# Two trunk layers with a mixture of experts on one core: gate and up by column tile, the gated rows transposed by VectorE

## What is computed

```python
def moe_ffn(h, router_w, router_bias, w_gate, w_up, w_down):
    ...
    hg = jnp.einsum('td,edf->tef', t, w_gate)
    hu = jnp.einsum('td,edf->tef', t, w_up)
    act = jax.nn.silu(hg) * hu * comb[:, :, None].astype(t.dtype)
    return jnp.einsum('tef,efd->td', act, w_down).reshape(B, L, D)
```

## Time and profile before

| | us |
|---|---|
| median of 3 runs | 1427.08 (1424.84 to 1427.25) |
| the profiled execution | 1437.77 |
| its span, first to last instruction | 1436.1 |
| TensorE busy in the span | 1110.4 (77%) |
| VectorE busy | 438.6 (31%) |
| ScalarE busy | 248.4 (17%) |
| GpSimd busy | 109.1 (8%) |
| HBM traffic over the span | 343.57 MB, mean 239 GB/s |

### The profile page before, as it was taken

One profiled execution on the slowest core, in us unless ns is written; L12 is line 12 of the kernel. 1 busy time (PEld: TensorE's weight loads), 2 busy tenths in 40 slices (PEclk: granted clock), 3 DMA queues, 4 the chain that ended last, 5 costly groups with the idle time before them and its releaser, 6 DMA issues.

```text
span 1436.1 us, 24771 instructions
## 1 busy us (share of the span) xinstructions
PE 1110.4 (77%) x9756; PEld 627.9 (44%) x9757; DVE 438.6 (31%) x1120; ACT 248.4 (17%) x456; POOL 109.1 (8%) x168
## 2 busy tenths in 40 slices
PE   1899996885579686889479998989739789877650
PEld 0444455535335343445245554444525455444320
DVE  0310137645112111222354233641522122222116
ACT  0301023303012111112221111110212121211101
POOL 1100000100100000001120000000010000000002
PEclk9999998995789888999889997989759999999975
DMA  9965233592575999781994015337322727599973
GB/s 325 366 226 201 99 125 133 222 381 113 225 306 223 419 422 422 323 322 41 387 375 160 35 59 202 121 118 292 118 95 83 327 95 301 217 408 415 421 315 132
DMA packets 96965, 343.57 MB, mean 239 GB/s; under 512 B 9926, under 2 KB 19081, under 8 KB 88732
## 3 DMA queue, kind: packets, MB, share of 16 engines
q1 hardware_dynamic: 69396, 289.19, 51.3%
q0 software_dynamic: 13152, 42.92, 8.4%
q10 hardware_dynamic: 14376, 10.89, 2.5%
HBM read 319.73 MB, written 23.23 MB: 239 GB/s over the span
## 4 chain that ended last, share of the span: by engine, by line
PE 47%; DMA 22%; DVE 11%; issue 10%; ACTq 5%; ACT 2%; SPq 2%; POOL 1%; DVEq 0%; POOLq 0%
PE bank L573 10%; DMA slot_rows<-arena 10%; PE bank L825 9%; PE bank L754 6%; PE bank L696 6%; ACTq L1068 5%; DMA arena<-in_moe_w_up_dram 4%; DMA ring<-in_ada_w_dram 4%; PE bank L739 4%; DMA ring<-in_moe_w_down_dram 3%; PE bank L748 2%; PE bank L526 2%; DVE arena L1160 1%; DVE arena L1141 1%; SPq L1176 1%
## 5 line engine op out<-in xcount | busy, mean ns | idle before, releaser
L739 PE MATMUL bank<-ring,arena 128*32 128x256 f32 x3008 | 198.2, 408 | 36.2 <-issue 24.2
L1063 ACT ACT_TABLE_LOAD x67 | 86.0, 1283 | 385.7 <-issue 370.8
L573 PE MATMUL bank<-ring,hT 128*128 128x512 f32 x336 | 144.9, 593 | 1.0 <-ACT hT L958 1.0
L739 PEld LDWEIGHTS bank<-ring,arena 128*32 128x32 f32 x3008 | 97.5, 116 | 110.0 <-issue 58.7
L748 PE MATMUL bank<-keep,arena 128*128 128x64 f32 x536 | 91.0, 294 | 64.1 <-DVE arena L1141 64.0
L825 PE MATMUL bank<-hT,ring 128*128 128x384 f32 x384 | 124.6, 487 | 1.0 <-ACT hT L958 1.0
L748 PEld LDWEIGHTS bank<-keep,arena 128*128 128x128 f32 x536 | 72.7, 197 | 110.3 <-DVE arena L1141 105.7
L739 PE MATMUL bank<-arena 128*32 128x256 f32 x1280 | 86.5, 416 | 17.7 <-DMA arena<-in_moe_w_up_dram 17.7
L573 PEld LDWEIGHTS bank<-ring,hT 128*128 128x128 f32 x336 | 63.6, 190 | 80.5 <-issue 79.3
L526 PE MATMUL bank<-ring,small 128*32 128x256 f32 x768 | 56.5, 459 | 53.4 <-DMA ring<-in_ada_w_dram 52.7
L754 PE MATMUL bank<-ring,arena 128*32 128x256 f32 x1504 | 95.0, 395 | 2.5 <-DMA ring<-in_moe_w_down_dram 2.5
(11 more groups left out here) (287 smaller groups left out, 1083.4 us busy)
## 6 DMA issues: line engine op xcount, KB each, us to landing
ring<-in_ada_w_dram SPq DMA_DIRECT2D x24, 2048.0 KB, 13.9
ring<-in_moe_w_gate_dram SPq DMA_DIRECT2D x22, 2048.0 KB, 17.2
ring<-in_moe_w_up_dram SPq DMA_DIRECT2D x22, 2048.0 KB, 16.7
ring<-in_moe_w_down_dram SPq DMA_DIRECT2D x22, 2048.0 KB, 20.4
arena<-in_moe_w_gate_dram SPq DMA_DIRECT2D x10, 2048.0 KB, 20.0
arena<-in_moe_w_up_dram SPq DMA_DIRECT2D x10, 2048.0 KB, 24.9
arena<-in_moe_w_down_dram SPq DMA_DIRECT2D x10, 2048.0 KB, 26.1
ring<-in_ev_w_in_dram SPq DMA_DIRECT2D x7, 2048.0 KB, 15.9
```

Of the source, the lines that this page charges most:

```text
L573: last = pe.matmul(bank[3 * (c % 2) + t], hT[:, k, t * P:(t + 1) * P], slot8(n)[:, k, :], start=k == 0, stop=k == KT - 1)
L739: last = pe.matmul(bank[1 + half][tile * BLK:(tile + 1) * BLK, 0:HALF], slot_inT[:, odd, pair, :], w[:, 2 * pair + odd, half * HALF:(half ...
L1063: act.activation(silu_g[:, 2 * half:2 * half + 2, :], bank[3 + half][:, 0:4 * BLK].rearrange("p (f s) -> p f s", f=2)[:, :, 0:BLK], ACT.Si ...
```

## The change

Each column tile of TensorE now takes 128 features of its own, both gate and up, over all eight groups of channels: a matmul's 256 columns are 128 of gate and 128 of up, from two places of the ring (`pair_of`). All of a block's gate and up is in bank 1, with nothing to add up afterwards: row 32 q + s has features 128 q to 128 q + 127 of slot s. ScalarE takes Silu of the whole 128 x 128 in one instruction, reading the features in the order (f, r) with feature = 128 q + 4 r + f. VectorE multiplies, and transposes the product in blocks of 32 x 32 (L1128 of the changed kernel), twice 128 x 64. Feature 128 q + 4 r + f then lies on partition 32 q + r, so w_down is now laid out `(p k) n` as well: partition p takes the 4 rows that lie next to each other. The copies of the 128 x 256 rows, the matmuls with `sides` and the constant itself are gone. `rows_in` now comes behind both halves of `gated`.

```diff
             src = a[("moe_w_gate", "moe_w_up", "moe_w_down")[j]][layer].rearrange("e d f -> (e d) f")
             rows = D if j < 2 else 512
-            src = src[bass.ds(e * rows, rows), :].rearrange("(p k) n -> p k n" if j < 2 else "(k p) n -> p k n", p=P)
+            src = src[bass.ds(e * rows, rows), :].rearrange("(p k) n -> p k n", p=P)
...
-            def gate_and_up(s, half, pair):
-
-                for side, w in enumerate((slot8(s), slot8(s + 1))):
-                    for odd in range(2):
-                        tile = 2 * side + odd
-                        last = pe.matmul(bank[1 + half][tile * BLK:(tile + 1) * BLK, 0:HALF], slot_inT[:, odd, pair, :],
-                                         w[:, 2 * pair + odd, half * HALF:(half + 1) * HALF], start=pair == 0, stop=pair == 3)
+            def gate_and_up(s, k):
+
+                both = pair_of(s)
+                for q in range(4):
+                    last = pe.matmul(bank[1][q * BLK:(q + 1) * BLK, 0:HALF], slot_inT[:, k % 2, k // 2, :],
+                                     both[:, :, k, q * P:(q + 1) * P], start=k == 0, stop=k == KT - 1)
                 return last
-
-            def features(b, half):
-
-                pe.wait_ge(S["gu_out"], b * 2 + (half + 1))
-                for f in range(2):
-                    at_f = half * HALF + f * P
-                    last = pe.matmul(bank[3 + half][:, f * 2 * BLK:(f + 1) * 2 * BLK], gu_rows[:, at_f:at_f + P], sides, start=True, stop=True)
-                last.then_inc(S["guT_mm"], 1)
...
                 pe.wait_ge(S["rowT"], b + 1)
-                for pair in range(4):
-                    last = gate_and_up(s, 0, pair)
+                for k in range(KT):
+                    last = gate_and_up(s, k)
                 last.then_inc(S["gu_mm"], 1)
-                gate_and_up(s, 1, 0)
-                gate_and_up(s, 1, 1)
-                features(b, 0)
-                gate_and_up(s, 1, 2)
-                gate_and_up(s, 1, 3).then_inc(S["gu_mm"], 1)
                 rows_to_channels()
-                features(b, 1)
...
-                for half in range(2):
-                    act.wait_ge(S["guT_mm"], b * 2 + (half + 1))
-                    act.activation(silu_g[:, 2 * half:2 * half + 2, :],
-                                   bank[3 + half][:, 0:4 * BLK].rearrange("p (f s) -> p f s", f=2)[:, :, 0:BLK],
-                                   ACT.Silu).then_inc(S["silu"], 1)
+                act.wait_ge(S["gu_mm"], b + 1)
+                act.activation(silu_g, bank[1][:, 0:P].rearrange("p (r f) -> p f r", f=FT), ACT.Silu).then_inc(S["silu"], 1)
...
-            def rows_out(b, half):
-                dve.wait_ge(S["gu_mm"], b * 2 + (half + 1))
-                dve.tensor_copy(gu_rows[:, half * HALF:(half + 1) * HALF], bank[1 + half][:, 0:HALF]).then_inc(S["gu_out"], 1)
-
             def gated(b, half):
-                up = bank[3 + half][:, 0:4 * BLK].rearrange("p (f s) -> p f s", f=2)[:, :, BLK:2 * BLK]
-                dve.wait_ge(S["silu"], b * 2 + (half + 1))
-                dve.tensor_tensor(act_T[:, 2 * half:2 * half + 2, :], silu_g[:, 2 * half:2 * half + 2, :], up, ALU.mult).then_inc(S["act"], 1)
+                up = bank[1][:, P:2 * P].rearrange("p (r f) -> p f r", f=FT)[:, 2 * half:2 * half + 2, :]
+                two = slice(2 * half, 2 * half + 2)
+                dve.tensor_tensor(act_rows[:, two, :], silu_g[:, two, :], up, ALU.mult).then_inc(S["gated"], 1)
+                dve.wait_ge(S["gated"], b * 2 + (half + 1))
+                dve.transpose(act_T[:, two, :].rearrange("p f s -> p (f s)"),
+                              act_rows[:, two, :].rearrange("p f s -> p (f s)")).then_inc(S["act"], 1)
...
             with dve.Fori(0, blocks) as b:
-                rows_out(b, 0)
+                dve.wait_ge(S["silu"], b + 1)
                 gated(b, 0)
-                rows_out(b, 1)
+                gated(b, 1)
                 dve.wait_ge(S["rowT_mm"], b + 2)
                 rows_in()
-                gated(b, 1)
```

More of the change, by code:

```diff
@@ L91 @@
 SLOT, FULL, PREVIOUS = ring_slots()
-K_ID, K_TRI, K_ONE, K_KEYG, K_KEYE, K_WF, K_LEFT, K_J, K_SIDE = 0, 128, 256, 384, 388, 404, 407, 408, 409
-K_N = 473
+K_ID, K_TRI, K_ONE, K_KEYG, K_KEYE, K_WF, K_LEFT, K_J = 0, 128, 256, 384, 388, 404, 407, 408
+K_N = 409
 M_RELF, M_RELB, M_MF, M_MB, M_XI, M_XB, M_RC, M_RS, M_DC, M_DS = (
@@ L116, in constants @@
     keep[:, K_J] = i
-    for side in range(2):
-        for s in range(BLK):
-            keep[[2 * side * BLK + s, (2 * side + 1) * BLK + s], K_SIDE + side * BLK + s] = 1
     mix = np.zeros((P, M_N))
@@ L209, in trunk_program @@
         ones = keep[:, K_ONE:K_ONE + P]
-        sides = keep[:, K_SIDE:K_SIDE + 2 * BLK]
         xf = x[:, :, :].rearrange("p t d -> p (t d)")
@@ L267, in trunk_program @@
         slot_inT = at(3328, 2, 4, BLK)
-        gu_rows = at(3584, 512)
-        silu_g = at(4096, FT, BLK)
+        silu_g = at(3584, FT, BLK)
+        act_rows = at(3712, FT, BLK)
         act_T = at(4224, FT, BLK)
@@ L349, in trunk_program @@
         MS = [{n: sem(f"{n}_{layer}") for n in (
-            "row_in", "rowT_mm", "rowT", "gu_mm", "gu_out", "guT_mm", "silu", "act", "down_mm", "slot_evac",
+            "row_in", "rowT_mm", "rowT", "gu_mm", "silu", "gated", "act", "down_mm", "slot_evac",
             "slot_stored")} for layer in range(2)]
@@ L406, in slot4, with pair_of @@
             return slot_of(n).rearrange("p (k n) -> p k n", k=FT)
+        def pair_of(n):
+            s = SLOT[n]
+            two = ring[:, s:s + 2, :].rearrange("p w c -> p (w c)") if s < RING else at(SPARE + (s - RING) * CHUNK, 2 * CHUNK)
+            return two.rearrange("p (w k n) -> p w k n", w=2, k=KT)
         def expert_matrix(sp, layer, e, s, j):
@@ L1181, in expert_through @@
                 if j < 2:
-                    sp.wait_ge(MS[layer]["gu_mm"], ends * 2)
+                    sp.wait_ge(MS[layer]["gu_mm"], ends)
                 else:
```

## The result

The changed kernel takes 1435.40 us (median of 8 runs, 1431.68 to 1439.59), the kernel before 1427.16 (8 runs, 1424.84 to 1428.37): a ratio of 1.0061, 95% interval 1.0044 to 1.0078, so **slower by 0.6%**, 8 us. The forecast was 1422.5: inside the range, on the wrong side. The profiled execution took 1439.59 us, with a span of 1437.8, 4.2 above its median.

What follows compares the result with a forecast made beforehand. Taken as bound: in quiet blocks a closed loop through stores, table load and Silu, in loaded blocks slow stores. Terms -14.3, -3, +21.2 and -8.5 sum to -4.6 us, giving a median of 1422.5; range 1403 to 1437.

Steps and rivals of the forecast that it cites:

- The closed loop of the quiet block: Blocks with no weights loading: eviction, stores, table load, Silu, `down`, eviction; 0.62 us less each, -14.3 us over 23.
- the whole new block: New order inside the expert blocks: -14.3 us in quiet blocks, -3 us in blocks that TensorE paces.
- rival 1: Slow stores also hold up the ring's refills, stretching the loading, and the kernel gets slower: 1433.5 us; chance 0.22.
- The pace: Every expert block under a long stretch of weight loading takes 12.1 us, its stores being slow throughout.
- The last block: End of layer 1, waiting for its down matrix: 10.6 us instead of 19.1, -8.5 us.
- Rivals 2 and 3: Stores as fast as now, 1401 us, chance 0.14; or VectorE's transpose dear, 1436.8 us, chance 0.04.
- rival 3: VectorE's transpose costs 0.85 us with its wait, so quiet blocks gain nothing: 1436.8 us; chance 0.04.
- rival 4: The weights set the end anyway; quiet-block gains turn into waiting for the next matrix: 1427 us; chance 0.10.
- the term on down's packets: w_down in 16 KB pieces slows stores in four long stretches of loading: +21.2 us; its load itself costs nothing.
- Short bursts of three matrices: Blocks beside brief loads of three matrices keep their times, their one store being slow already: put at nothing.
- The long stretches: Four runs of blocks under loading, from 460, 1110, 1242 and 1310 us: +9.7, +1.2, +4.0, +6.3, together +21.2 us.
- the five blocks from 1242: A stretch of loading late in the kernel: 10.5 us, three blocks at 12.1, one at 6.9, so +4.0 us.

Runs made afterwards that it cites:

- the control: The kernel before, unchanged, run and profiled once more: 1426.30 us, ratio 0.9991.

## Why the prediction was wrong

**What held.** The closed loop of the quiet block: each of its steps came within 0.05 us, and with the 4 KB pieces back the quiet blocks gave -13.4 for a forecast -14.3, the whole new block 15.8 us in the total for a forecast 14.3 + 3. The packets: w_down in 16 KB is served like gate and up, and its load alone costs nothing (the loading from about 457 to 602 us ends at the same time, so rival 1's stretched refills didn't come, although its 1433.5 lies within 2 us of the result). The pace: eleven blocks from 461.96 to 594.76 take 12.07 us each, forecast 12.1. The last block took 8.4 us, forecast 10.6, and q1 had 1.51 MB beside 0.44 on q0 from 1384 to 1389 us, 77% for a forecast four fifths. That down landed at 1389.6, forecast 1385 to 1390, is partly luck: it was issued at 1358.8, 5 us later than before and not up to 4 earlier, and landed 30.8 us after that instead of 39.7. The last two row vectors on q0 were issued only at 1387.2 and 1387.8, before at 1379.0 and 1379.5, 14 us ahead of the landing. Rivals 2 and 3 fell by the slow stores and the 0.24 us transpose, although rival 3's 1436.8 lies nearest of all to the result; of rival 4 nothing showed, as what was won in quiet blocks stayed won.

**What failed** is one sentence of the term on down's packets: "Short bursts of three matrices keep their times, since their one slow store is slow already." A burst (gate, up and down of one expert; the one of 620.7 us has landed at 639.1) outlasts a loaded block of 12 us, and its down part is now 16 KB pieces too. The first block's stores in it landed in 7.8 us in the median and 8.8 at most in the kernel before (issued from 614 to 621 us), and in 8.5 and 10.6 now (from 624 us). The block that starts at 624.25 us went from 10.8 to 12.6, and the two from 1292 from 10.4 and 7.5 to 12.0 and 11.7 us.

Two blocks behind a burst, quiet before (7.6 each), took 9.2 and 9.5, and not by a store's landing. In the first of them:

```profile
438.86 0.42 DVE L1142 COPY arena<-bank 128x256 f32<-128x256 f32 x1 [2.13 <-DMA slot_rows<-arena]
439.46 2.72 ACTq L1052 DMA_DIRECT2D slot_rows<-arena  x4
...
444.67 3.25 PE L747 MATMUL bank<-ring,arena 128*32 128x256 f32 x32 [1.74 <-DVE arena L1128]
...
448.09 0.42 DVE L1142 COPY arena<-bank 128x256 f32<-128x256 f32 x1 [2.78 <-PE bank L747]
```

Issuing the four stores takes 2.72 us (2.94 in the other block) instead of 1.75, which moves Silu, and `down` takes 3.25 (3.31) instead of 1.93. TensorE's clock for this `down` and for that of the quiet block above (bounds, length, busy, clock, DMA share, GB/s):

```profile
444.67:447.92 3.25, 3.25 (x36) 0.58 0.11 40
664.52:666.45 1.93, 1.93 (x36) 1.00 0.22 68
```

The 0.58 is a mean between the clock's two levels, near the lower (1.2 of 2.4 GHz). The engine had stood idle for 1.04 us and for 1.74 us before this `down`. The first is a wait for rows fetched on q0, of which the prediction said that they are "wanted a block later". Together the two effects are the 4.9 us that the two blocks lost against 6.94, and the prediction has no term for either, though it named the first as a way to fall: "The forecast also falls if ScalarE's table load moves". Why the issue took longer, no run shows.

Against the profile of before this is +5.8 for the two blocks from 1292, 5.9 lost in the quiet blocks, and 3.9 in the short bursts where -3 was forecast: 15.6 us that had been put at nothing (19.3 against the control's profile, 19.6 against the kernel with w_down in 4 KB). The long stretches were over-priced in return, 15.6 measured for 21.2 (in the last one the two blocks from 1292 had taken the loss), and the last block gave 2.2 more. -4.6 + 15.6 - 5.6 - 2.2 = +3.2, the table's sum. That the five blocks from 1242 came near their forecast (+5.5 for +4.0) is luck: with w_down in 4 KB they still took 54.1 us for the 49.7 of before.

The prediction's range for its own mechanism has a slip too: from 1422.5 its bounds, +4.6 and +8, reach 1435 and not 1433.

How the medians' 8 us divide stays open: the blocks have +3.2 against one profile of before and +9.6 against the other. The start of the experts, +4.3 to +4.9 in the profiles, had no term of its own; but the kernel with 4 KB in the first experts alone gained nothing by having it back, so I don't call it a cost shown.

The rule of the Trainium skill (DMA: Bandwidth & Descriptors, Queues, rings and completion order), a whole packet in turn from each queue, agrees with the profiles where two queues have work throughout: from 285 to 290 us 117 packets on q1 beside 121 on q0 with 16 KB pieces, and 272 beside 272 in the kernel before with everything in 4 KB. What the forecast lacked was its full reach. It was applied where blocks stood in long stretches, and not to each store and each small load that shares time with a 16 KB piece. The layout that saves a transposition on one engine was bought with a slower queue on another, and both effects were of one size, 16 and 22 us.

## What to carry to other kernels

A layout change of a weight is a change to every small transfer that runs beside it: look at bytes per packet on the big queue, and price each small DMA that is under way at the same time, in short bursts too. Where a loop waits for the landing of small stores, cut the large loads into pieces of 4 KB or so (here -4% against the changed kernel, for a few lines), and check at which size the large loads themselves begin to slow. Compare block by block and take a second profile of the kernel before, since one execution can be 10 us off.

## What was not expected of the hardware

- Normalization rows on q0 were slowed by the weights' piece size in the same way as the stores: VectorE's wait for them went from 20.1 to 31.5 us, and is 14.2 with all three matrices in 4 KB. The router's 48 matmuls then started from 334.8 to 344.9 us, in the two profiles of before from 332.7 or 333.5 to 340.8.
- A moving operand with every fourth element (16 bytes apart) takes 631 ns per record for 128 x 256, with neighbouring elements 408.
- The `down` of a block behind a burst ran at a granted clock of 0.58, in 3.25 us instead of 1.93 at 1.00; TensorE had idled 1.04 and 1.74 us just before.
- 2 KB pieces move 0.387 MB per us, 8 KB pieces 0.422, with q1 nearly alone in both.
